# Two more units of hgrn's input weights kept between the two hgrn phases, in slots of the gather ring

## What is computed

```python
def hgrn2(xn, w_in, lower_bound, out_gain, w_out):
    q, f, i, g = jnp.split(xn @ w_in, 4, axis=-1)        # w_in: 1024 x 4096
    ...                                                   # 8 heads, chunks of 64 tokens
    return o.reshape(B, S, D_MODEL).astype(xn.dtype) @ w_out

def peer_ffn(xn, w_q, sub_keys, u_tab, v_tab):
    ...
        expert = i1 * PEER_N_KEYS + i2                    # 8 heads x 16 experts for each token
        gates = jax.nn.softmax(cv, axis=-1)
        u = u_tab[expert]
        act = jax.nn.gelu(jnp.einsum('pd,phkd->phk', xb, u).astype(jnp.float32), approximate=False)
        return jnp.einsum('phk,phkd->pd', (gates * act).astype(xb.dtype), v_tab[expert])
```

## Time and profile before

| | us |
|---|---|
| median of 3 runs (1463.78 to 1466.13) | 1464.59 |
| the profiled execution | 1463.57 |
| its span, first to last instruction | 1461.6 |
| PE busy | 1276.9 |
| DVE busy | 1060.2 |
| ACT busy | 633.8 |
| POOL busy | 612.0 |

### The profile page before, as it was taken

How to read it: one execution, slowest core, us unless ns; L and a number is a source line. 1 busy time by engine, 2 the same in 40 slices (tenths; PEclk the granted TensorE clock), 3 DMA queues, 4 the chain that set the end, 5 groups by cost and what they waited for, 6 DMA issues and landing times.

```text
span 1461.6 us, 15133 instructions
## 1 busy us (share of the span) xinstructions
PE 1276.9 (87%) x4672; PEld 704.3 (48%) x4672; DVE 1060.2 (73%) x2537; ACT 633.8 (43%) x1919; POOL 612.0 (42%) x520
## 2 busy tenths in 40 slices
PE   9998988888876989889897699998999789878876
PEld 5564444344543757455454465745445444422222
DVE  4688877756796787777598778787758967674545
ACT  3345444354543253345454335334455443443334
POOL 0254554454444344336344334433545544434442
PEclk9999998999998999999999999999999899999999
DMA  9899999999999999999999999999999999999997
GB/s 390 352 408 420 420 420 421 421 420 421 421 421 421 404 422 394 423 421 406 423 421 421 423 388 419 421 421 422 421 421 421 422 420 421 421 421 419 422 421 300
DMA packets 83824, 603.45 MB, mean 413 GB/s; under 512 B 9696, under 2 KB 10016, under 8 KB 12832
## 3 DMA queue, kind: packets, MB, share of 16 engines
q0 software_dynamic: 74016, 536.90, 88.8%
q1 hardware_dynamic: 9440, 65.24, 10.7%
q10 hardware_dynamic: 288, 0.34, 0.1%
HBM read 601.40 MB, written 1.05 MB: 412 GB/s over the span
## 4 chain that ended last, share of the span: by engine, by line
DMA 40%; PE 35%; DVE 13%; ACT 9%; issue 2%; POOL 0%; DVEq 0%; POOLq 0%; ACTq 0%
DMA ring<-experts,idx 40%; PE acc L1614 21%; DVE ring L1195 7%; PE rbank L1564 3%; ACT diag L600 2%; PE ab L1486 2%; ACT L722 2%; PE ab L1489 1%; ACT coef L600 1%; ACT L716 1%; ACT gel L722 1%; DVE h L1204 1%; PE ab L1339 1%; PE cbank L1502 1%; PE acc L1377 1%
## 5 line engine op out<-in xcount | busy, mean ns | idle before, releaser
L1614 PE MATMUL acc<-ring,diag 128*128 128x512 f32 x1768 | 879.5, 626 | 172.9 <-ACT diag L600 163.0
L580 POOL DMA_INDIRECT ring<-experts,idx x510 | 606.6, 1189 | 827.0 <-PE acc L1614 655.3
L1195 DVE CUSTOM_DVE_ANT_0 ring<-ring,xn 128x1024 f32<-128x1024 f32 x512 | 623.9, 1220 | 266.7 <-DMA ring<-experts,idx 263.8
L1614 PEld LDWEIGHTS acc<-ring,diag 128*128 128x128 f32 x1768 | 319.2, 196 | 551.9 <-ACT diag L600 288.8
L722 ACT ACTIVATE gel<-dots 128x1 f32<-128x1 f32 x512 | 103.3, 202 | 710.2 <-DVE dots L1195 709.7
L600 ACT ACTIVATE diag<-ident_gain,coef 128x128 f32<-128x128 f32 x442 | 177.6, 402 | 14.5
L600 ACT ACTIVATE coef<-gate,gel 128x1 f32<-128x1 f32 x512 | 151.0, 295 | 25.3 <-DVE h L1204 9.0
L1564 PEld LDWEIGHTS rbank<-xTs,wroute 128*128 128x128 f32 x832 | 112.9, 195 | 54.2 <-issue 53.2
L1564 PE MATMUL rbank<-xTs,wroute 128*128 128x128 f32 x832 | 114.3, 279 | 0.0
L1204 DVE SCALAR_TENSOR_TENSOR h<-ring,coef,h 128x1024 f32<-128x1024 f32 x69 | 88.5, 1282 | 4.6 <-ACT coef L600 4.4
L1486 PEld LDWEIGHTS ab<-xTs,wmix 128*128 128x128 f32 x352 | 45.9, 192 | 11.1 <-issue 10.6
(11 more groups left out here) (295 smaller groups left out, 1012.8 us busy)
## 6 DMA issues: line engine op xcount, KB each, us to landing
wmix<-hgrn_in SPq DMA_DIRECT2D x19, 1024.0 KB, 9.4
wroute<-route_w SPq DMA_DIRECT2D x8, 2304.0 KB, 13.2
ring<-experts,idx POOLq DMA_INDIRECT x510, 14.8
wmix<-hgrn_out SPq DMA_DIRECT2D x7, 1024.0 KB, 9.4
wroute<-hgrn_in SPq DMA_DIRECT2D x5, 1024.0 KB, 13.5
wmix<-attn_out SPq DMA_DIRECT2D x4, 1024.0 KB, 16.4
ring<-attn_in SPq DMA_DIRECT2D x6, 384.0 KB, 5.8
ring<-attn_in SPq DMA_DIRECT2D x3, 768.0 KB, 8.5
```

Of the source, the lines that this page charges most:

```text
L580: pool.indirect_dma_start(out=ring[:, k * 2 * D:(k + 1) * 2 * D], out_offset=None, in_=experts, in_offset=bass.IndirectOffsetOnAxis(ap=idx ...
L1195: dve.tensor_tensor_reduce(out=u_rows(k), in0=u_rows(k), in1=xn[:, tile], scale=1.0, scalar=0.0, op0=ALU.mult, op1=ALU.add, accum_out=dots ...
L1614: last = nc.tensor.matmul(acc[:, j * HALF:(j + 1) * HALF], diag[:, m % DIAGS], v_rows(k)[:, j * HALF:(j + 1) * HALF], start=opens_sum(n), ...
```

## The change

`UNIT_KEPT` gets two more entries: unit 26 is unit 6 and unit 27 is unit 7, so SP loads six units in p = 2 and not eight. For that the second tile's heads go 3, 2, 1, 0.

- **Unit 6** stays in place 0 of `wmix` until p = 2. The other units of both phases have only places 1 and 2 there for that time.
- **Unit 7** gets place 9, a slot of the ring (`LONG_SLOT`). SP loads it after row 28 of p = 1 has been added; POOL gets the slot back with row 68 of p = 2, when `h_proj` has reached 28 (unit 27 done).
- **Unit 14** goes into the second part of pair 1 in `wroute` (place 8). In rows 88 to 91 of p = 1 ACT copies it in four parts of 128 x 512 into another slot of the ring (`LENT_SLOT`), once row 85 has been added; unit 18 reads it there. POOL gets that slot back with row 26 of p = 2, when `h_proj` has reached 19. The load of pair 1 waits for this copy too (`unit_lent`).
- The ring is then a list of slots that are taken from the front and given back at the end (`ring_slots`). Its slots in use are 8 up to row 35 of p = 1; from row 36 a gather waits for the row seven before it, from row 92 for the row six before it; from row 27 of p = 2 again seven, from row 69 again eight.
- Of the loads that remain, unit 11 stands at SP's row 42 (39 before), unit 24 at 39 (22 before), unit 25 at 42, units 28, 29 and 30 at 52, 56 and 59.

```diff
-UNIT_PLACES = 8
+UNIT_PLACES = 10
 MOVED_UNIT, MOVED_PLACE = 15, 7
+LENT_UNIT, LENT_PLACE = 14, 8
+LONG_UNIT, LONG_PLACE = 7, 9
-    return i if tile == 0 else (3, 2, 0, 1)[i]
+    return i if tile == 0 else (3, 2, 1, 0)[i]
+LAST_LENT, BACK_ROW = PER + FIRST_LEND - 3, 2 * PER + 26
+LAST_LONG, LONG_BACK_ROW = PER + 28, 2 * PER + 68
+
+def ring_slots():
+    slots, ordinals, earlier = [], [], []
+    order = [(k + 6) % RING for k in range(RING)]
+    last, used, lent, lent_long = [None] * RING, [0] * RING, None, None
+    for n in range(PHASES * PER):
+        if n == BACK_ROW:
+            order.insert(0, lent)
+        elif n == LONG_BACK_ROW:
+            order.insert(0, lent_long)
+        k = order.pop(0)
+        if n == LAST_LENT:
+            lent = k
+        elif n == LAST_LONG:
+            lent_long = k
+        else:
+            order.append(k)
+        used[k] += 1
+        slots.append(k)
+        ordinals.append(used[k])
+        earlier.append(last[k])
+        last[k] = n
+    return slots, ordinals, earlier, lent, lent_long
-UNIT_PLACE = (0, 1, 2, 0, 1, 2, 0, 1, 5, 6, 2, 0, 3, 4, 1, 7,
-              3, 4, 1, 7, 5, 6, 2, 0, 1, 2, 0, 1, 2, 0, 1, 2)
-UNIT_KEPT = {16: 12, 17: 13, 18: 14, 19: 15, 20: 8, 21: 9, 22: 10, 23: 11}
+UNIT_PLACE = (0, 1, 2, 0, 1, 2, 0, 9, 5, 6, 2, 1, 3, 4, 8, 7,
+              3, 4, 8, 7, 5, 6, 2, 1, 2, 1, 0, 9, 2, 1, 0, 2)
+UNIT_KEPT = {16: 12, 17: 13, 18: 14, 19: 15, 20: 8, 21: 9, 22: 10, 23: 11, 26: 6, 27: 7}
-              1: {12: 3, 15: 4, 19: 5, 22: 6, 32: 7, 33: 8, 34: 9, 35: 10, 39: 11, 59: 12, 60: 13, 62: 14, 63: 15},
-              2: {22: 24, 39: 25, 42: 26, 52: 27, 56: 28, 59: 29, 62: 30, 72: 31}}
+              1: {12: 3, 15: 4, 19: 5, 22: 6, 32: 7, 33: 8, 34: 9, 35: 10, 42: 11, 59: 12, 60: 13, 62: 14, 63: 15},
+              2: {39: 24, 42: 25, 52: 28, 56: 29, 59: 30, 72: 31}}
...
+                elif place == LONG_PLACE:
+                    sp.wait_ge(slots_free, tensor_rows(LAST_LONG) + 1)
...
                     sp.wait_ge(unit_moved, MOVES)
+                    sp.wait_ge(unit_lent, MOVES)
...
-                if n >= RING and vector_row(n - RING):
-                    pool.wait_ge(v_added, vector_rows(n - RING) + 1)
+                if n == BACK_ROW:
+                    pool.wait_ge(h_proj, LENT_UNIT + 5)
+                elif n == LONG_BACK_ROW:
+                    pool.wait_ge(h_proj, LONG_UNIT + 21)
+                elif n >= RING and vector_row(EARLIER[n]):
+                    pool.wait_ge(v_added, vector_rows(EARLIER[n]) + 1)
                 elif n >= RING:
-                    pool.wait_ge(slots_free, tensor_rows(n - RING) + 1)
+                    pool.wait_ge(slots_free, tensor_rows(EARLIER[n]) + 1)
...
+                if p == 1 and FIRST_LEND <= q < FIRST_LEND + MOVES:
+                    s = slice((q - FIRST_LEND) * 2 * D // MOVES, (q - FIRST_LEND + 1) * 2 * D // MOVES)
+                    if q == FIRST_LEND:
+                        act.wait_ge(whgrn_in[LENT_PLACE], 16)
...
+                    copy(lent_weights[:, s], unit_weights(LENT_PLACE)[:, s]).then_inc(unit_lent, 1)
...
-                dve.wait_ge(slot_in[k], 16 * (n // RING + 1))
+                dve.wait_ge(slot_in[k], 16 * ORDINALS[n])
...
+                            elif c == 0 and k == 0 and x == LENT_UNIT + 4:
+                                pe.wait_ge(unit_lent, MOVES)
```

More of the change, by code:

```diff
@@ L58 @@
 HEAD_EXP = (115, 124)
-MOVES, FIRST_MOVE = 4, 96
+MOVES, FIRST_MOVE, FIRST_LEND = 4, 96, 88
 RESIDUAL = 32
@@ L139, in heads_at @@
 def heads_at(tile, i):
-    return i if tile == 0 else (3, 2, 0, 1)[i]
+    return i if tile == 0 else (3, 2, 1, 0)[i]
 def hgrn_out_loads(n):
     return n + 1 if n < ITERS else n
+LAST_LENT, BACK_ROW = PER + FIRST_LEND - 3, 2 * PER + 26
[22 more added lines that the diff above has]
+    return slots, ordinals, earlier, lent, lent_long
+SLOTS, ORDINALS, EARLIER, LENT_SLOT, LONG_SLOT = ring_slots()
 def unit_part(x):
     return x % 4 // 2, x % 2
-UNIT_PLACE = (0, 1, 2, 0, 1, 2, 0, 1, 5, 6, 2, 0, 3, 4, 1, 7,
-              3, 4, 1, 7, 5, 6, 2, 0, 1, 2, 0, 1, 2, 0, 1, 2)
-UNIT_KEPT = {16: 12, 17: 13, 18: 14, 19: 15, 20: 8, 21: 9, 22: 10, 23: 11}
+UNIT_PLACE = (0, 1, 2, 0, 1, 2, 0, 9, 5, 6, 2, 1, 3, 4, 8, 7,
+              3, 4, 8, 7, 5, 6, 2, 1, 2, 1, 0, 9, 2, 1, 0, 2)
+UNIT_KEPT = {16: 12, 17: 13, 18: 14, 19: 15, 20: 8, 21: 9, 22: 10, 23: 11, 26: 6, 27: 7}
 UNIT_LOADS = {0: {40: 0, 61: 1, 82: 2},
-              1: {12: 3, 15: 4, 19: 5, 22: 6, 32: 7, 33: 8, 34: 9, 35: 10, 39: 11, 59: 12, 60: 13, 62: 14, 63: 15},
-              2: {22: 24, 39: 25, 42: 26, 52: 27, 56: 28, 59: 29, 62: 30, 72: 31}}
+              1: {12: 3, 15: 4, 19: 5, 22: 6, 32: 7, 33: 8, 34: 9, 35: 10, 42: 11, 59: 12, 60: 13, 62: 14, 63: 15},
+              2: {39: 24, 42: 25, 52: 28, 56: 29, 59: 30, 72: 31}}
 def unit_load(x):
@@ L376, in trunk @@
         h_on_ready, h_oT_ps, h_oT_ready = sem("h_on_ready"), sem("h_oT_ps"), sem("h_oT_ready")
-        h_outproj, unit_moved = sem("h_outproj"), sem("unit_moved")
+        h_outproj, unit_moved, unit_lent = sem("h_outproj"), sem("unit_moved"), sem("unit_lent")
         r_proj, r_qT, r_score, r_top = sem("r_proj"), sem("r_qT"), sem("r_score"), sem("r_top")
@@ L396, in unit_weights @@
                 return wroute[:, 1, 0:2 * D]
+            if place == LENT_PLACE:
+                return wroute[:, 1, 2 * D:4 * D]
+            if place == LONG_PLACE:
+                return ring[:, LONG_SLOT * 2 * D:(LONG_SLOT + 1) * 2 * D]
             pair, at_ = ITERS - 1 - (place - UNIT_HOMES) // 2, (place - UNIT_HOMES) % 2
             return wroute[:, pair, at_ * 2 * D:(at_ + 1) * 2 * D]
+        lent_weights = ring[:, LENT_SLOT * 2 * D:(LENT_SLOT + 1) * 2 * D]
         def slot_of(n):
-            return (n + 6) % RING
+            return SLOTS[n]
         def u_rows(k):
@@ L465, in load_unit @@
                     sp.wait_ge(h_proj, last_use_of_place(x) + 1)
-                elif place == MOVED_PLACE:
+                elif place == LONG_PLACE and vector_row(LAST_LONG):
+                    sp.wait_ge(v_added, vector_rows(LAST_LONG) + 1)
+                elif place == LONG_PLACE:
+                    sp.wait_ge(slots_free, tensor_rows(LAST_LONG) + 1)
+                elif place in (MOVED_PLACE, LENT_PLACE):
                     sp.wait_ge(r_score, CHUNKS + 4)
@@ L766, in beside @@
                         hgrn(tile, i, q - HEAD - HGRN_PERIOD * i)
+                if p == 1 and FIRST_LEND <= q < FIRST_LEND + MOVES:
+                    s = slice((q - FIRST_LEND) * 2 * D // MOVES, (q - FIRST_LEND + 1) * 2 * D // MOVES)
+                    if q == FIRST_LEND:
+                        act.wait_ge(whgrn_in[LENT_PLACE], 16)
+                        if vector_row(LAST_LENT):
+                            act.wait_ge(v_added, vector_rows(LAST_LENT) + 1)
+                        else:
+                            act.wait_ge(slots_free, tensor_rows(LAST_LENT) + 1)
+                    copy(lent_weights[:, s], unit_weights(LENT_PLACE)[:, s]).then_inc(unit_lent, 1)
                 if p == 1 and FIRST_MOVE <= q < FIRST_MOVE + MOVES:
@@ L1473, in project @@
                     place = UNIT_PLACE[x]
-                    w = (mix[:, 0:2 * D] if x == MOVED_UNIT + 4 else unit_weights(place)).rearrange("p (k c) -> p k c", k=KT // 2)
+                    home = mix[:, 0:2 * D] if x == MOVED_UNIT + 4 else lent_weights if x == LENT_UNIT + 4 else unit_weights(place)
+                    w = home.rearrange("p (k c) -> p k c", k=KT // 2)
                     for c in range(3):
```

## The result

| | before | after |
|---|---|---|
| median (lowest to highest) of 12 runs, us | 1464.12 (1463.21 to 1466.13) | 1467.91 (1465.94 to 1471.39) |
| ratio, 95% interval | | 1.0028 (1.0020 to 1.0035) |
| the profiled execution | 1463.57 | 1468.7 |
| its span | 1461.6 | 1466.8 |

The forecast was 1462.8 us, in a range from 1459.4 to 1466.0. The kernel became slower by about 3.8 us (2.9 to 5.1 by the interval of the ratio), and the time lies outside the range.

A forecast was written before the change was run, and what follows sets the result against it. It took DMA bandwidth as the bound, 2.48 us per mebibyte, with PE and ring depth limiting some stretches. -4.97 + 2.5 + 0.7 = -1.8 us took the median from 1464.59 to 1462.8 us, range 1459.4 to 1466.0.

The forecast's parts named there:

- The two loads: Two 1 MiB unit loads of p = 2 fall away, 2.48 us each, and come back in full: -4.97 us.
- Rows 36 to 40 of p = 2: With seven slots the gathers leave later, row 39 lands 2.5 us behind, and the lag counts in full: +2.5 us.
- Rows 87 and 88 of p = 1: With seven slots row 88 leaves at 659.79 and lands late: +0.7 us, from 0 to 1.9.
- The other rows of p = 1 with seven slots: Given no loss of their own; outside the rows named, even six slots' 14.9 us turn was held to cover 10.4 needed.
- The six slots: Rows 92 of p = 1 to 26 of p = 2: row 119 lands on time without margin, so nothing.
- The copies: Four ACT copies of 0.61 us behind rows 88 to 91 of p = 1 fit ACT's idle time: 0, at most 2.5 us.
- SP's queue: SP's wait for row 28 before unit 7 precedes the old wait, and units behind it wait for later events anyway: nothing.
- POOL's waits on `h_proj`: At the two rows where a slot comes back, units 18 and 27 are done about when POOL arrives or earlier: nothing.
- Six slots don't carry the end of p = 1: Rival, chance 0.12: flights 1.5 us longer at low depth make four PE-paced stretches late, 6 us more, 1468.8 us.
- The saving comes in full: Rival, chance 0.27: the other engines may take up the lag, giving 1459.6 us, or up to 1461 with part of it.
- Nothing saved: Rival, chance 0.11: PE's chain sets the pace of p = 2, loads were covered, only lags remain: 1464.6 to 1467.8 us.
- The Trainium skill: Its rule estimates a 4.4 us flight for 1 MiB, giving losses of 0.9 and 0 and 1460.5 us; not used.

The follow-up runs named there:

- e11: Kernel before, all 24 loads, two slots set aside only from rows 84 and 85 of p = 1 to 26 and 27 of p = 2: 1470.20 us.
- e9: Kernel before, all 24 loads, one ring slot set aside only from row 28 to row 75 of p = 1: 1465.43 us.
- e1: Kernel before with the change's ring, both slots set aside but holding nothing, all 24 loads, no copies: 1473.33 us.
- e2: Kernel after, its loads and heads kept, but all eight slots in the ring and no ACT copies (some products wrong): 1458.98 us.
- e10: Kernel before, all 24 loads, one ring slot set aside only from row 20 to row 67 of p = 2: 1466.45 us.
- e6: Kernel after without the four ACT copies of unit 14 and the waits on them, slot still set aside (unit 18's product wrong): 1467.55 us.
- e7: Kernel before with DVE's dot product replaced by a plain one-operand sum, leaving out the product with the token: 1460.66 us.

## Why the prediction was wrong, step by step

The step that failed is the cost of the missing slots. The sum had nothing for the six slots of rows 92 of p = 1 to 26 of p = 2, which cost 6.3 us alone (e11), and nothing for rows 36 to 84 of p = 1, which cost 1.5 alone (e9). It had 3.2 us for all missing slots, where e1 measured 9.5. The saving was right.

- **The two loads, -4.97: right.** e2 measured -4.9, and after's trace shows 2.5 and 2.1 at the two places named.
- **Rows 36 to 40 of p = 2, +2.5: right.** e10 alone measured +2.5, after's trace 2.0. Rows 36 to 39 leave when the step said, each at the time at which the next row left before, 5.4 us on. They flew 5.3 to 5.5 us and not 5.9, which is why the trace shows the smaller loss:

```profile
872.56 0.94 POOL L628 DMA_INDIRECT ring<-experts,idx  x1 [3.67 <-PE acc L1674]
875.59 0.94 POOL L628 DMA_INDIRECT ring<-experts,idx  x1 [2.09 <-PE acc L1674]
879.75 0.94 POOL L628 DMA_INDIRECT ring<-experts,idx  x1 [3.22 <-PE acc L1674]
882.36 0.94 POOL L628 DMA_INDIRECT ring<-experts,idx  x1 [1.67 <-PE acc L1674]
```

- **Rows 87 and 88 of p = 1, +0.7: too low by about half.** After loses 1.5 from row 72 to 96; the 0.9 counted from row 64 has 0.6 that was made good on the way. Nor is it a loss of its own, as the sum had it: with eight slots the same rows are where an earlier lag is made good (e9).
- **The other rows of p = 1 with seven slots, not in the sum: wrong.** Between rows 20 and 64 after lost 3.5 us, and the slot missing in rows 36 to 75 costs 1.5 by itself (e9). The sum went by rows 36 to 40 of p = 2 and 87 and 88 of p = 1, and left these at nothing without a reason. What shows them was in the trace of before: of the four low slices that the prediction names (404, 394, 406, 388 GB/s in the earlier trace rows) the second is this stretch, where PE is busy for 10.00 of 10.00 us and the DMA down to 320 GB/s (570 to 580 us, above).
- **The six slots, 0: wrong, and the term that decided.** The price alone is +6.3 (e11); in after it is 2.8 by the dots. Why it is less there no run shows: a part may have been lost already in the rows before. Two numbers failed. The need of a turn, 10.4 us, was taken from p = 3, where PE has time; where PE is busy for 10.00 of 10.00 us, a row first waits for its dot, and then for PE. And the flight of 5.9 us was taken from the quietest place. Two gathers of after, rows 118 and 119 of p = 1, in POOL, and their times to landing:

```profile
746.61 1.25 POOL L628 DMA_INDIRECT ring<-experts,idx  x1 [2.57 <-PE acc L1674]
750.12 1.26 POOL L628 DMA_INDIRECT ring<-experts,idx  x1 [2.25 <-PE acc L1674]
```

```profile
DMA to landing us min/median/max: 7.3/7.3/7.3
...
DMA to landing us min/median/max: 7.6/7.6/7.6
```

They flew 7.3 and 7.6 us. Row 118's slot had been filled at 738.45 (row 112), its dot started at 741.32, PE freed it at 746.34, its gather left at 746.61, and it was full again at 753.9. That is 2.9 us of waiting for its dot, 5.3 from the dot to the issue and 7.3 of flight, 15.4 us (unrounded), where 6 x 2.48 = 14.9 is all that six slots allow. The step had 0 for the first, 4.5 for the second and 5.9 for the third. Row 119's turn took 16.8, and its dot waited for it:

```profile
757.73 1.23 DVE L1252 CUSTOM_DVE_ANT_0 ring<-ring,xn 128x1024 f32<-128x1024 f32 x1 [1.01 <-DMA ring<-experts,idx]
```

The forecast itself said of row 119 that it lands on time "with no margin". A term with no margin isn't 0: its bounds were 0 and several microseconds, and they belonged in the range.
- **The copies, SP's queue and POOL's waits on `h_proj`, 0: right.** For the copies by e6; for SP's queue by e2, which has after's order of loads and gains in full; for POOL's waits by after's trace, where POOL doesn't wait for PE at either row. The gather of row 68 of p = 2 (the one of row 26, at 842.20, has the same 0.30 us before it):

```profile
966.84 0.94 POOL L628 DMA_INDIRECT ring<-experts,idx  x1 [0.30 <-issue]
```

- **The rivals.** *Six slots don't carry the end of p = 1* is what happened. It asked for 1.5 us more flight in four stretches; rows 118 and 119 flew 1.4 and 1.7 longer, four places lost, and its 1468.8 stands beside 1467.9. Part of that is luck: it put the early loss of p = 1 in rows 28 to 40, where the trace has 2.7 of the 3.5 us behind row 62, and it kept the flights of rows 36 to 40 of p = 2 long, which were the shortest of all. It had 0.12, since I held against it a flight of 6.0 us in p = 2, another place with another load. *The saving comes in full* is wrong for the kernel, though right for the loads. *Nothing saved* fell with e2: PE is busy for 87% of the span and a load fewer is still worth its 2.48 us. (By the weights given, "faster" has 0.05 + 0.27 = 0.32, not 0.31.)
- **The Trainium skill.** Shortest flights of after are those of rows 36 to 40 of p = 2 (5.3 us, by the view of the row at 872.56); the trace doesn't agree with the estimated 4.4 us that came from "DMA: Bandwidth & Descriptors", section "Anatomy of one DMA — SWDGE (gpsimd) path", and less still at rows 118 and 119. By that rule the loss would have been smaller (876.94 + 4.4 against 880.3 is 1.0 us, where the prediction has 0.9), and it was larger.

## What to carry to other kernels

A buffer in a ring is bandwidth lent to the time when another engine is slow: before one is taken for something else, add up release, issue, flight and the wait for use in the slowest stretch, not in the steady one, and compare with slots times pace. A turn that comes out at the limit had a price here, and where a full ring would make a lag good later, the missing slot costs there too. Split such a change by its parts: here one kept unit gains 2.0 us, and the second one turns that into a loss of 3.8.

## What the hardware showed that was not expected

**POOL's issue of a gather waits for DVE.** With a two-operand operation of DVE under way, the issue of an indirect DMA, 0.94 us otherwise, lasts up to 2.0 us, and 2.72 with two in a row; with a one-operand sum of the same length (1214 ns beside 1220) the mean is 972 ns instead of 1189, and the kernel before is 3.7 us faster (e7; it also does without the 82 ns in which the accumulator is read). The Trainium skill, "SBUF — State Buffer", section "Who interferes with whom", says that a DVE instruction with two SBUF inputs contends with a GpSimd instruction that reads SBUF; the trace agrees, for an issue that reads its indices there. That the ports are the cause no run shows by itself; the runs show that it goes with the kind of the DVE operation.

**The granted clock falls at other places from run to run.** In e10 and e11 the dots of p = 2 lose another 2.2 and 2.3 us between rows 25 and 26, which no step explains and no gather makes (DVE doesn't wait for a landing there). Before, e10 and e11 at the same rows:

```profile
840.00:850.00 10.00, 8.65 (x41) 5.32 (x40) 7.74 (x18) 5.09 (x16) 5.24 (x4) 1.00 1.01 416
```

```profile
840.24:850.24 10.00, 9.41 (x27) 4.68 (x26) 6.30 (x15) 4.16 (x13) 3.30 (x3) 0.66 1.01 417
```

```profile
848.84:858.84 10.00, 9.18 (x26) 4.64 (x25) 6.19 (x15) 4.18 (x13) 3.04 (x4) 0.66 1.01 417
```

With 0.66 granted, some 6.8 of the 10 us were at 1.2 GHz, and PE got 27 and 26 matmuls done, not 41. PE's timeline has the place. Before and e10, the same four matmuls of one row's addition:

```profile
842.54 1.98 PE L1614 MATMUL acc<-ring,diag 128*128 128x512 f32 x4 [1.35 <-ACT diag L600]
```

```profile
842.75 3.78 PE L1645 MATMUL acc<-ring,diag 128*128 128x512 f32 x4 [0.59 <-ACT diag L631]
```

That is 1.8 us of the 2.2, and the ten matmuls behind them take 1.76 us in place of 1.28. What PE did ahead of it doesn't tell the three apart: in the 10 us before it was busy 6.90 us at a clock of 0.94 in the kernel before, 7.88 at 0.83 in e10 and 6.41 at 0.99 in e11. Just before a stretch in which PE sets the pace, it is a loss that stays. It is a part of why these two profiled executions lie above their medians, by 1.6 and 4.3 us (e11's was also 3.3 us late by row 20 of p = 1), and a trace's own time has to be read with that in mind.
